# Turning the convolution's inputs with VectorE and a DRAM scratch instead of TensorE transposes, in a two-layer hybrid decoder

## What is computed

```python
qk = silu(causal_depthwise_conv(concatenate([mq, mk], axis=-1), conv_w, conv_b))
mq, mk = split(qk, 2, axis=-1)
# causal_depthwise_conv: y[t, c] = b[c] + sum over j of w[j, c] * x[t - 3 + j, c]
h = mlstm_chunkwise(heads(mq), heads(mk) * MLSTM_HEAD_DIM ** -0.5, heads(mv), ig, lf)
x = layer_norm(alpha * x + mix @ w_out, ln_g, ln_b)
```

## Time and profile before

| | before |
|---|---|
| median of 3 runs | 1271.84 us (1271.75 to 1272.41) |
| span of the profiled execution | 1269.9 us |
| TensorE busy | 1257.0 us, 99% |
| VectorE busy | 893.0 us, 70% |
| ACT busy | 705.4 us, 56% |
| GpSimd busy | 244.0 us, 19% |
| the 64 transposes of L639 | 0.87 us a group of eight in the chain |

### The profile page before, as it was taken

The page is one execution under the profiler, slowest core; times in us unless marked ns, Lnnn a source line. Parts: engine busy times, 40 slices in busy tenths (PEclk is TensorE's granted clock), DMA queues, the critical chain, the costliest instruction groups (busy, mean ns, idle before and its releaser), DMA issues.

```text
span 1269.9 us, 16388 instructions
## 1 busy us (share of the span) xinstructions
PE 1257.0 (99%) x6342; PEld 1040.2 (82%) x6342; DVE 893.0 (70%) x1229; ACT 705.4 (56%) x989; POOL 244.0 (19%) x268
## 2 busy tenths in 40 slices
PE   9999999999999999999999999999999999999996
PEld 8888888878888888888888788888888888888885
DVE  5686876876667655865785779768665776567656
ACT  5477476575555544444563775666755555345441
POOL 0321522522220000400003223334131200004000
PEclk9999999999999999999999999999999999999998
DMA  9968768765665555465657587678546556565562
GB/s 336 310 209 261 236 189 277 260 192 164 204 195 174 184 186 185 152 230 190 207 186 238 183 282 245 193 258 282 184 149 215 183 157 209 165 197 198 186 212 86
DMA packets 129277, 264.97 MB, mean 209 GB/s; under 512 B 8824, under 2 KB 8976, under 8 KB 128688
## 3 DMA queue, kind: packets, MB, share of 16 engines
q1 hardware_dynamic: 123712, 247.23, 60.6%
q0 software_dynamic: 3680, 13.28, 3.0%
q10 hardware_dynamic: 1808, 3.42, 0.7%
HBM read 258.61 MB, written 5.28 MB: 208 GB/s over the span
## 4 chain that ended last, share of the span: by engine, by line
PE 86%; ACT 4%; DVE 4%; POOL 3%; issue 2%; DVEq 0%; POOLq 0%; ACTq 0%
PE ps L373 79%; ACT arena L810 2%; DVE w_lo L1060 2%; ACT w_hi L736 2%; PE ps L444 1%; PE ps L671 1%; PE ps L391 1%; PE ps L639 1%; POOL arena L1684 1%; PE ps L533 0%; POOL arena L1680 0%; PE ps L518 0%; ACT arena L807 0%; PE ps L355 0%; DVE arena L1133 0%
## 5 line engine op out<-in xcount | busy, mean ns | idle before, releaser
L1060 DVE TENSOR_TENSOR w_lo<-w_raw,w_hi 128x1024 fp32r<-128x1024 f32 x408 | 527.1, 1305 | 326.4 <-ACT w_hi L736 324.5
L736 ACT ACTIVATE w_hi<-w_raw 128x1024 fp32r<-128x1024 f32 x408 | 427.3, 1058 | 388.9 <-PE ps L373 339.3
L373 PE MATMUL ps<-w_hi,xT_hi 128*128 128x512 f32 x1616 | 636.2, 394 | 0.7 <-DVE w_lo L1060 0.7
L373 PE MATMUL ps<-w_hi,xT_lo 128*128 128x512 f32 x1616 | 629.6, 390 | 0.0
L373 PE MATMUL ps<-w_lo,xT_hi 128*128 128x512 f32 x1616 | 629.0, 389 | 0.0
L373 PEld LDWEIGHTS ps<-w_hi,xT_hi 128*128 128x128 f32 x1616 | 303.4, 188 | 64.3 <-issue 1.3
L373 PEld LDWEIGHTS ps<-w_hi,xT_lo 128*128 128x128 f32 x1616 | 303.3, 188 | 64.0
L373 PEld LDWEIGHTS ps<-w_lo,xT_hi 128*128 128x128 f32 x1616 | 303.6, 188 | 61.4
L292 POOL TENSOR_TENSOR carried<-ident 1x1 f32<-1x1 f32 x30 | 19.6, 652 | 454.8 <-DVE arena L1416 178.7
L1217 DVE CUSTOM_DVE_ANT_0 mix<-xres,mix 128x1024 f32<-128x1024 f32 x64 | 89.0, 1390 | 1.1
L807 ACT ACTIVATE arena<-arena 32x256 f32<-32x256 f32 x128 | 53.2, 416 | 15.6 <-DVE arena L1137 14.0
(11 more groups left out here) (244 smaller groups left out, 825.3 us busy)
## 6 DMA issues: line engine op xcount, KB each, us to landing
w_raw<-w_in_dram SPq DMA_DIRECT2D x367, 512.0 KB, 4.5
w_raw<-w_out_dram SPq DMA_DIRECT2D x64, 512.0 KB, 4.8
mix<-gate_w_dram SPq DMA_DIRECT2D x32, 512.0 KB, 5.6
xres<-x_dram ACTq DMA_DIRECT2D x4, 512.0 KB, 8.4
v_dram<-arena POOLq DMA_DIRECT2D x4, 512.0 KB, 6.3
z<-v_dram POOLq DMA_DIRECT2D x8, 256.0 KB, 5.6
z<-ln_g_dram POOLq DMA_DIRECT2D x2, 1024.0 KB, 7.7
store<-ln_b_dram POOLq DMA_DIRECT2D x2, 1024.0 KB, 7.9
```

The costliest lines, as they stand in the source:

```text
L373: mm = pe.matmul(ps[2 * s + t][:], a[:, order[c] * KC + k, t * P:(t + 1) * P], b[:, k], start=(c + k + i == 0), stop=(c == CH - 1 and k == ...
L736: A(hi_of(n, c), w_raw[:, c % RING], ACT.Copy).then_inc(w_hi_done, 1)
L1060: TTn(lo_of(n, c), w_raw[:, c % RING], hi_of(n, c).bitcast(F32), ALU.subtract).then_inc(w_lo_done, 1)
```

## The change

VectorE takes over the turning. Its transpose works in squares of 32x32, so the pieces have to be moved between partitions afterwards; that is done by a store to a DRAM scratch (`conv_dram`) and four loads back, all on SP's queue. For each convolution i the steps are now: both takes; one VectorE transpose of all 1024 elements a partition into `conv_zT` (semaphore `conv_turned`); SP stores it (`put`); SP loads it, with channels on partitions, into `conv_T` (`fetch`, semaphore `conv_moved`). There the 256 time steps stand in eight pieces of 32, each with four places ahead of it, of which VectorE fills three with the end of the piece before (zeros in the first). ACT and VectorE then do the same scaled copy, taps and SiLU, reading `conv_T` in SBUF in place of PSUM. Ahead of the convolution ACT and VectorE split the rest of the running block and chunks 0 and 1 of the next one; chunks 2 and 3 of the next block stand between the halves. SP's `put` stands behind the load of a block's last chunk, its `fetch` behind the second load of the next block. TensorE's transposes are gone; the wait at the scores is unchanged.

```diff
+        conv_zT = arena[:, 4096:5248].rearrange("p (f b x) -> p f b x", f=4, x=HALO + QUARTER)
+        conv_T = arena[:, 5248:6400].rearrange("p (b m x) -> p b m x", b=SEQ // QUARTER, x=HALO + QUARTER)
+        conv_dram = nc.dram_tensor("conv_dram", (DEPTH, 4, 4, TT, 4, QUARTER, 4 * (HALO + QUARTER)), F32, kind="Internal").ap()
...
 SyncE
+                def put(i):
+                    sp.wait_ge(conv_turned, l * 4 + i + 1)
+                    dst = conv_dram[l, i].rearrange("f t u j x -> (u j) (f t) x")
+                    src = conv_zT.rearrange("p f (t m) x -> p (f t) (m x)", t=TT)
+                    sp.dma_start(dst, src).then_inc(conv_put, 16)
+                def fetch(i):
+                    sp.wait_ge(conv_put, (l * 4 + i + 1) * 16)
+                    src = conv_dram[l, i].rearrange("f t u j x -> f j (t u) x")
+                    dst = conv_T.rearrange("p b m x -> p b (m x)")
+                    for f in range(4):
+                        sp.dma_start(dst[f * QUARTER:(f + 1) * QUARTER], src[f]).then_inc(conv_moved, 16)
...
+                        if c == 1 and N_CONV + 2 <= n <= N_CONV + 5:
+                            fetch(n - N_CONV - 2)
+                        if c == CH - 1 and N_CONV + 1 <= n <= N_CONV + 4:
+                            put(n - N_CONV - 1)
...
 TensorE
-                    chunks(N_CONV + i, Q_CONV + i, i % 2, 0, 2)
-                    conv_transposes(i - 1)
-                    chunks(N_CONV + i, Q_CONV + i, i % 2, 2, 6)
+                    chunks(N_CONV + i, Q_CONV + i, i % 2, 0, 6)
...
-                chunks(N_MV, Q_MV, 0, 0, 2)
-                conv_transposes(3)
-                chunks(N_MV, Q_MV, 0, 2, CH)
+                chunks(N_MV, Q_MV, 0, 0, CH)
...
 ACT
+                split(N_CONV + 1, 0, 4)
                 for i in range(4):
                     n = N_CONV + 1 + i
-                    split(n, 0, 4)
                     take(n, i % 2, z[:, i % 2, 0, :])
-                    split(n, 4, 6)
-                    act.wait_ge(conv_ps, l * 4 + i + 1)
+                    split(n, 4, 8)
+                    split(n + 1, 0, 2)
+                    act.wait_ge(conv_moved, (l * 4 + i + 1) * 4 * 16)
                     for hf in range(2):
                         for t in range(2):
                             m = 4 * i + 2 * hf + t
-                            y = A(conv_y[:, hf, t, :], ps[4 + hf][:, t * SEQ:(t + 1) * SEQ], ACT.Identity,
+                            y = A(conv_y[:, hf, t, :].rearrange("p (b s) -> p b s", s=QUARTER),
+                                  conv_T[:, :, 2 * hf + t, HALO:], ACT.Identity,
                                   bias=cb[:, m:m + 1], scale=cw[:, m, 3:4])
                         y.then_inc(conv_bias, 1)
                     for hf in range(2):
-                        split(n, 6 + hf, 7 + hf)
+                        split(n + 1, 2 + hf, 3 + hf)
...
 VectorE
+                split(N_CONV + 1, 0, 4)
                 for i in range(4):
                     n = N_CONV + 1 + i
-                    split(n, 0, 2)
+                    take(n, i % 2, z[:, i % 2, 1, :])
+                    dve.wait_ge(z_act, taken_act(l, Q_CONV + i))
+                    dve.wait_ge(z_dve, taken_dve(l, Q_CONV + i))
+                    V.transpose(conv_zT.rearrange("p f b x -> p b f x")[:, :, :, HALO:],
+                                z[:, i % 2].rearrange("p t c -> p (t c)")).then_inc(conv_turned, 1)
+                    split(n, 4, 6)
...
-                    split(n, 2, 4)
-                    take(n, i % 2, z[:, i % 2, 1, :])
+                    split(n, 6, 8)
+                    split(n + 1, 0, 2)
+                    dve.wait_ge(conv_moved, (l * 4 + i + 1) * 4 * 16)
+                    V.memset(conv_T[:, 0, :, 1:HALO], 0.0)
+                    own(V.tensor_copy(conv_T[:, 1:, :, 1:HALO], conv_T[:, :-1, :, QUARTER + 1:]))
                     for hf in range(2):
-                        split(n, 4 + 2 * hf, 6 + 2 * hf)
                         dve.wait_ge(conv_bias, l * 8 + 2 * i + hf + 1)
                         for j, back in ((2, 1), (1, 2), (0, 3)):
                             for t in range(2):
                                 m = 4 * i + 2 * hf + t
-                                y = conv_y[:, hf, t, back:SEQ]
-                                f = STT(y, ps[4 + hf][:, t * SEQ:(t + 1) * SEQ - back], cw[:, m, j:j + 1], y,
-                                        ALU.mult, ALU.add)
+                                y = conv_y[:, hf, t, :].rearrange("p (b s) -> p b s", s=QUARTER)
+                                f = STT(y, conv_T[:, :, 2 * hf + t, HALO - back:HALO - back + QUARTER], cw[:, m, j:j + 1],
+                                        y, ALU.mult, ALU.add)
+                        split(n + 1, 2 + hf, 3 + hf)
```

More of the change, by code:

```diff
@@ L38 @@
 RES = 4
+QUARTER = P // 4
+HALO = 4
 LEN = SEQ // RES
@@ L236, in hybrid_layers @@
         sgu_ps, sgu_done = sem("sgu_ps"), sem("sgu_done")
-        conv_ps, conv_bias, conv_done, conv_silu = (
-            sem("conv_ps"), sem("conv_bias"), sem("conv_done"), sem("conv_silu"))
+        conv_turned, conv_put, conv_moved, conv_bias, conv_done, conv_silu = (
+            sem("conv_turned"), sem("conv_put"), sem("conv_moved"), sem("conv_bias"), sem("conv_done"), sem("conv_silu"))
         ag_silu, mg_silu, mo_sigmoid = sem("ag_silu"), sem("mg_silu"), sem("mo_sigmoid")
@@ L1402, in _ @@
                                 m = 4 * i + 2 * hf + t
-                                y = conv_y[:, hf, t, back:SEQ]
-                                f = STT(y, ps[4 + hf][:, t * SEQ:(t + 1) * SEQ - back], cw[:, m, j:j + 1], y,
-                                        ALU.mult, ALU.add)
+                                y = conv_y[:, hf, t, :].rearrange("p (b s) -> p b s", s=QUARTER)
+                                f = STT(y, conv_T[:, :, 2 * hf + t, HALO - back:HALO - back + QUARTER], cw[:, m, j:j + 1],
+                                        y, ALU.mult, ALU.add)
                             own(f) if j else f.then_inc(conv_done, 1)
+                        split(n + 1, 2 + hf, 3 + hf)
                 n = N_MV + 1
-                split(n, 0, 4)
+                dve.wait_ge(conv_done, (l + 1) * 8)
                 dve.wait_ge(mix_att, l + 1)
```

## The result

The changed kernel takes **1277.45 us**, the median of its runs (1275.6 to 1279.95), against 1271.8 before on the same chip: a ratio of 1.0045, with an interval of 1.0030 to 1.0059, so it is slower. The forecast was 1268.2. The case that came is rival 1, a round trip slower than a lap allows, priced at 1277.6; it came with less waiting than that price held and with a cost that stood in no case.

A forecast was written before the change was run, and what follows sets the result against it. TensorE was taken as the bound, busy 1257.0 of 1269.9 us. 1269.9 - 7.2 (transposes) + 3.6 (two stalls) = 1266.3 for the span; the runs' median lies 1.9 above, so 1268.2 us, range 1264.6 to 1279.

The forecast's parts named there:

- rival 1: Turned inputs arrive too late, delaying the last convolution over two or three laps; 1277.6 us, slower; chance 0.28.
- lap: From one turned input's arrival through copies, taps, splits and next turn to the next arrival: 10.3 us plus transfer, against 21.76.
- What is taken away: TensorE's eight groups of eight transposes, two layers: 0.9 us each, 7.2 us off TensorE (7.0 to 7.4).
- The line to the last SiLU: Serial work from chunk 1's split through halo and taps to the last SiLU; stalls TensorE 1.8 us per layer.
- S + 1.8: S is when TensorE reaches a layer's first mLSTM score; the last SiLU was forecast 1.8 us after it.
- bounds in the sum: Limits on the time from a stall of 1.4 to 2.6 us at the first score: 1267.2 to 1269.8 us.
- Rival 2: Small prices before the last SiLU add up: stall 3 to 4 us per layer, 1270.6 to 1272.6 us; chance 0.12.
- The store: SP's write of the turned input, 590 KB in 576-byte rows, to DRAM: forecast 3.3 us.
- D = 10: Time from the end of VectorE's turn to the turned input's arrival: 10 us, ends at 7.5 and 17.
- The limit of 11.4: Longest turn-to-arrival time, in us, at which convolutions keep pace with TensorE's blocks; beyond it each block slips by the excess.
- the loads' wait on SP for chunk 2: SP's wait before loading back holds next block's chunk 2 weights some 3 us; forecast to cost nothing.
- S - 7.9: Earliest start of chunk 1's split on ACT: 7.9 us before TensorE reaches a layer's first mLSTM score.

## Why the prediction was wrong, step by step

- **What is taken away: right.** 7.2 us were forecast; leaving the transposes out of the kernel before takes 7.4 off the span, and the kernel with later scores loses 7.3 (1269.9 to 1262.6).
- **The line to the last SiLU: right.** S + 1.8 was forecast, a stall of 1.9 and 1.6 came in the kernel with light loads and in the one without the round trip. (Of the bounds in the sum one is a slip: a stall of 1.4 gives 1267.4, not 1267.2.) Its small terms came as sized: the turn 1.25 (1.24), a halo of 0.07 + 0.19 (0.3), six taps in 2.7 at 482 ns each (476 to 480). Rival 2 had nothing to stand on.
- **The store: nearly right**, 3.7 against 3.3.
- **D = 10, and waits for the DMAs at nothing: the step that failed.** D measured 12.0 to 13.5 over both layers. I put *one* weight load of 1.6 between store and loads. The queue has two: SP issues chunks 0 and 1 of the next block at 448.57 and 449.7, while the store is still in flight. The diff says it, `fetch` behind `c == 1`. At the same place (i = 3, first layer) D is 8.6 with both light, 10.1 with one in front and 12.4 with two: store, loads and one weight load were sized about right, and their number was wrong. But the count is not all of it. With one in front D was the forecast's, and the stalls were 5.4 and 4.7 all the same, since the weight load displaced behind the four loads came late; the sum had nothing for that on either side. Neither run that changed the place in the queue cured it. SP's queue took 57.9% of the engines in this stretch before, and from 415 to 482 us after, where I had some 74:

```profile
q1 hardware_dynamic: 10021, 13.47, 69.3%
```

- **The limit of 11.4: the form right, the number 0.4 high.** From the arrival at 436.65 to the end of the next turn at 447.44 it takes 10.8, not 10.3; the half microsecond is spread over handovers and taps, a tenth at a time. That puts the limit at 11.0, and the slip of the last lap at D = 12.0 is the measured 1.0; in the second layer 10.8 + 13.5 is the measured 24.3. At D = 8.6 nothing slips, with the store twice all laps do. What the rule leaves out is that a weight load can set the lap as well: 23.32 at a D under the limit, with chunk 1 issued behind the four loads.
- **The weights' own lateness: missed.** The prediction looked at the loads' wait on SP for chunk 2 only, and put it at nothing. ACT's waits for the weights of chunks 0 and 1 (8.8 us in this stretch of the first layer, in four waits; 4.1 in two in the kernel without the store) stand on the same line: these loads are issued behind the store. In the changed kernel ACT starts the split of chunk 1 at 456.94, 6.5 before TensorE stands at the score (463.44), where the prediction had S - 7.9. That is 1.4 late, so with the last input in time the stall of 4.8 would still have been some 3.2 (1.8 + 1.4, an estimate from these rows).
- **A stall costs more than its length: missed.** No term of the sum, and no rival, had the clock. It is 4.5 of the 8.2 us of the profiled execution. Without it the stalls and restarts would have left 10.1 + 0.5 - 7.2 = 3.4 us, hardly slower. Rival 1's 1277.6 was met by chance in part: it held stalls of 6.5 us a layer from D = 13.5; measured are 4.8 and 5.4 from D of 12.0 to 13.5, and the clock made up the rest.
- **The chances.** Rival 1 had 0.28 against 0.55, on a margin of 1.4 us in D whose ends were 7.5 and 17. The estimate from the Trainium skill (DMA: Bandwidth & Descriptors, "Anatomy of one DMA"), D about 7, was too low even for the round trip with light loads in front (8.6). The argument that two transfers of nearly that size took 2.7 and 3.3 us weighed a store with nothing beside it and the fastest of 37 weight loads, whose median is 4.3.

## What to carry to other kernels

Work taken off the bounding engine counts only as long as its replacement, round trip and all, is done when that engine asks: write down the lap (landing, work, turn, transfer) against the block, and count every transfer that the issuing queue puts in between, and ask of each one that is moved behind who waits for it then. Where the lap is tight, let the bounding engine ask later; here three chunks of other work in front of the scores turned 1277.45 us into 1265.07, and nothing had to become faster. Price a stall of TensorE by its length and by the clock behind it.

## What the runs showed of the hardware

TensorE's granted clock stayed full over waits of 1.6 and 1.9 us and was 0.50 to 0.57 of full (0.50 is 1.2 GHz) in the first stretch after waits of 4.4 to 5.4 us. It was full again 3.8 us after the restart at the first stall of the changed kernel (468.22 to 472.0) and some 6 us after it at the second (1100.71 to about 1107), so stalls of much the same length cost differently. The two groups right behind a stall took 1.9 to 3.2 us longer than the next ones, 0.26 of it the restart. A turn of 128 x 1024 elements through DRAM, store and four loads of 590 KB in rows of 576 bytes, takes 8.6 us from the end of VectorE's transpose with no heavy transfer in between, 10.1 with one load of 512 KB in between and 12.0 to 13.5 with two. A queue of its own did not make the loads land sooner (10.1 us against 8.6 from the first issue).
